# Work moved ahead of waits in a three-layer fp32 transformer kernel on one core, and decay terms on row halves

## The reference

```
# first block: eight heads of 64, T5 bias; gates; convolved feed-forward of 2816
mod = silu(c) @ ada_w + ada_b                     # 1024 x 6144, six modulation vectors
q, k, v, p, g_attn, g_pool = split((norm(x) * (1 + scale1) + shift1) @ w_in)
merged = sigmoid(g_attn) * (attn @ w_branch_attn) + sigmoid(g_pool) * (pool @ w_branch_pool)
x = x + gate1 * (merged @ w_out)
x = x + gate2 * ((silu(conv(h2 @ w_gate)) * conv(h2 @ w_value)) @ w_down)
# even layer: 8 forgetting heads and 8 sliding-window heads with sinks, then a swiglu
fq, fk, fv, fgl, sq, sk, sv = split(h @ w_in)
cum = cumsum(log_sigmoid(fgl + forget_b))         # per head, over tokens
s = fq @ fk.T / 8 + cum[query] - cum[key]         # the decay terms of a forgetting head
x = x + g_m * (concat(o_fox, o_swa) @ w_out);  x = x + g_f * swiglu(h)
# odd layer: 16 heads, each query keeps its 64 best keys by an index score, then 8 experts, top 2
q, k, v, iq, ik, iw = split(h @ w_in)             # q, k, iq, ik are rotated by position
score = sum over heads of iw * relu(iq @ ik.T);  keep top 64 keys of each query
x = x + g_m * (o @ w_out);  x = x + g_f * mixture_of_experts(h)
return rms_norm(x)
```

## Time and profile before

| | us |
|---|---|
| median of 3 runs | 1267.29 (1265.4 to 1267.48) |
| the profiled execution's own time | 1263.85 |
| span of that execution | 1262.2 |
| PE busy | 1229.3 (97%) |
| DVE busy | 671.6 (53%) |
| ACT busy | 277.8 (22%) |
| POOL busy | 88.5 (7%) |

### The profile page before, as it was taken

How to read it: one execution, slowest core, us unless ns; L and a number is a source line. 1 busy time by engine, 2 the same in 40 slices (tenths; PEclk the granted TensorE clock), 3 DMA queues, 4 the chain that set the end, 5 groups by cost and what they waited for, 6 DMA issues and landing times.

```text
span 1262.2 us, 26659 instructions
## 1 busy us (share of the span) xinstructions
PE 1229.3 (97%) x10620; PEld 936.9 (74%) x10620; DVE 671.6 (53%) x1672; ACT 277.8 (22%) x739; POOL 88.5 (7%) x157
## 2 busy tenths in 40 slices
PE   6999999999999999999999999999999999999997
PEld 4758888999999767789999997776654455455445
DVE  5455563888888735546776777883541011101104
ACT  4332203212111414540000004275300000000001
POOL 0100000000000000000000000100021100110120
PEclk9999999999999999999999999999999999999999
DMA  9999884577777583146777785795599999999993
GB/s 355 414 399 412 334 283 149 176 273 269 267 276 277 199 314 103 34 167 217 260 277 278 269 316 186 296 375 128 222 383 396 420 399 397 400 422 399 397 399 151
DMA packets 74822, 368.78 MB, mean 292 GB/s; under 512 B 8740, under 2 KB 8996, under 8 KB 49979
## 3 DMA queue, kind: packets, MB, share of 16 engines
q1 hardware_dynamic: 56594, 271.22, 57.3%
q0 software_dynamic: 18160, 96.64, 20.2%
HBM read 347.76 MB, written 20.06 MB: 291 GB/s over the span
## 4 chain that ended last, share of the span: by engine, by line
PE 92%; DVE 3%; DMA 2%; ACT 1%; SPq 1%; issue 1%; DVEq 0%
PE banks L957 21%; PE banks L697 16%; PE banks L1283 13%; PE banks L944 12%; PE banks L1332 9%; PE banks L1307 5%; PE banks L722 4%; PE banks L826 2%; PE banks L786 2%; PE banks L1024 2%; PE banks L881 1%; DMA side<-ada 1%; PE banks L865 1%; DMA ring<-stream 1%; PE banks L894 1%; DVE side L1728 1%
## 5 line engine op out<-in xcount | busy, mean ns | idle before, releaser
L1728 DVE CUSTOM_DVE_ANT_0 side<-side 128x1024 f32<-128x1024 f32 x128 | 151.1, 1220 | 32.6 <-DMA side<-ada 32.5
L1283 PE MATMUL banks<-ring,arena 128*32 128x512 f32 x1536 | 166.3, 592 | 1.6 <-DVE arena L2244 1.6
L944 PE MATMUL banks<-arena,ring 128*128 128x256 f32 x704 | 158.6, 379 | 0.0
L944 PEld LDWEIGHTS banks<-arena,ring 128*128 128x128 f32 x704 | 130.7, 190 | 16.1
L697 PE MATMUL banks<-h,ring 128*128 128x256 f32 x640 | 141.8, 380 | 0.3
L1283 PEld LDWEIGHTS banks<-ring,arena 128*32 128x32 f32 x1536 | 51.5, 110 | 111.4 <-issue 110.2
L697 PEld LDWEIGHTS banks<-h,ring 128*128 128x128 f32 x640 | 120.4, 190 | 18.4 <-issue 2.2
L2347 DVE TENSOR_TENSOR arena<-arena,banks 128x256 f32<-128x256 f32 (+1 forms) x48 | 15.2, 330 | 179.0 <-ACT arena L1665 178.9
L697 PE MATMUL banks<-arena,ring 128*128 128x256 f32 x384 | 84.3, 380 | 0.7 <-ACT arena L1464 0.5
L957 PEld LDWEIGHTS banks<-h,ring 128*128 128x128 f32 x672 | 81.4, 192 | 2.2
L614 POOL DMA_DIRECT2D side<-ada x64 | 34.0, 532 | 687.7 <-DVE msum L1728 678.2
(11 more groups left out here) (332 smaller groups left out, 1553.3 us busy)
## 6 DMA issues: line engine op xcount, KB each, us to landing
ring<-stream SPq DMA_DIRECT2D x247, 512.0 KB, 5.5
ring<-experts SPq DMA_DIRECT2D x96, 1024.0 KB, 18.9
side<-ada POOLq DMA_DIRECT2D x64, 1024.0 KB, 7.6
side<-experts SPq DMA_DIRECT2D x24, 1024.0 KB, 20.5
arena<-experts SPq DMA_DIRECT2D x8, 1024.0 KB, 21.9
yrows<-side POOLq DMA_DIRECT2D x1, 6144.0 KB, 42.7
hrows<-side POOLq DMA_DIRECT2D x1, 5632.0 KB, 23.4
arena<-lasts SPq DMA_DIRECT2D x8, 512.0 KB, 22.2
```

The lines of the kernel that those rows point to most:

```text
L944: last = pe.matmul(banks[:, 4 + c // 2, (c % 2) * T:(c % 2 + 1) * T], ring[:, s, c * P:(c + 1) * P], hid[:, j % 2, :], start=first and c % ...
L1283: ins = pe.matmul(banks[BLOCK * j:BLOCK * (j + 1), t, :], hg[:, t, k, :], ring[:, m, (j % 2) * 512:(j % 2 + 1) * 512], start=(k == 0), sto ...
L1728: dve.tensor_tensor_reduce(weights, weights, cond[:, 0 if layer0 else 1, :], 1.0, 0.0, ALU.mult, ALU.add, accum_out=msum[:, n:n + 1]).then ...
```

## The change

1. In `raw_units`, two blocks of the second raw unit stand ahead of the norm's sums. A whole normed unit (`fq` 2, `iq` 1) stands ahead of the few columns (`fgl`, `iw`), and the next one (`fq` 3, `iq` 2) ahead of their turning; ACT's takes follow in that order.
2. The wait for the two `fv` units moves from before the scores to the first product with values.
3. The decay terms contract over 40 rows: the even head of a pair on rows 0 to 39, the odd one on rows 64 to 103, with instructions of the two heads in turn. `sel` has four columns of heads in place of eight, each with the two heads of a pair; `lf72` becomes `lfs` with 104 columns, at a place of its own.
4. PE's `attend` has one order for all three attentions: the first transpose ahead of the other units of a step, except at the last steps, where they stand ahead of it. Of the last step's units, the first goes ahead of the values, the rest behind. The last early output block is split in two halves for that. In the first attention, ACT takes the second head's exponents after the transposed copy as in the others, and its other steps follow them, save at the last steps.
5. `take_query` copies the query out of PSUM first and makes the shifted copies from SBUF.
6. `rows_turned` of the first expert pass stands ahead of the copy of `pickT`.

```
--- before.py
+++ after.py
@@ -46,6 +46,7 @@
 HIDS = 2 * BLOCKS
+FORGET = 104
 EXTRA = (2 * T) // (CAP + 1)
@@ -157,10 +158,10 @@
     add(("stat", 2))
+    add(("fq", 2), 1)
     add("fgl")
-    add(("fq", 2), 1)
+    add(("fq", 3), 1)
     add("fglT")
-    add(("fq", 3), 1)
     add_all("fk", 4)
@@ -173,10 +174,10 @@
     add(("stat", 4))
+    add(("iq", 1), 1)
     add("iw")
-    add(("iq", 1), 1)
+    add(("iq", 2), 1)
     add("iwT")
-    add(("iq", 2), 1)
     add(("iq", 3), 1)
@@ -305,10 +306,10 @@
         sqT, skT, sv = region(12, [4, T]), region(16, [T]), region(17, [2, P])
-        sel = region(18, [8, T], 72)
+        sel = region(18, [4, T], FORGET)
         lf = region(26, [3, 2, 8])
-        lf72 = region(26.25, [2, 72])
-        cum = region(27, [T], 72)
+        lfs = region(22, [2, FORGET])
+        cum = region(27, [T], FORGET)
         ropet = region(29, [3, T])
@@ -797,17 +798,19 @@
                     raw_block(a.bank, a.pos, r, k)
+                for k in range(2):
+                    raw_block(b.bank, b.pos, r, k)
                 begin(U["stat", r])
...
                     raw_block(a.bank, a.pos, r, k)
-                for k in range(2):
+                for k in range(2, 4):
                     raw_block(b.bank, b.pos, r, k)
                 norm_spread(r)
-                for k in range(2, KC):
+                for k in range(4, KC):
                     raw_block(b.bank, b.pos, r, k)
 
-            def early_out(name, moving, pairs_done, k):
+            def early_out(name, moving, pairs_done, k, columns=range(4)):
 
@@ -816,7 +819,7 @@
                     pe.wait_ge(s_o, pairs_done + k + 1)
-                    for c in range(4):
+                    for c in columns:
                         out_block(name, moving, c, k)
@@ -868,9 +871,13 @@
                     for a in pair:
-                        for lo, hi, n in ((0, HALF, HALF), (HALF, TRI, T)):
-                            ins = pe.matmul(banks[:, score_bank(a.n), lo:hi], cum[:, n - HALF:n], sel[:, a.i, 0:n],
-                                            start=False, stop=bool(lo))
+                        rows = slice(64 * a.half, 64 * a.half + 40)
+                        ins = pe.matmul(banks[:, score_bank(a.n), 0:HALF], cum[rows, 0:HALF], sel[rows, a.chunk, 0:HALF],
+                                        start=False, stop=False)
+                    for a in pair:
+                        rows = slice(64 * a.half, 64 * a.half + 40)
+                        ins = pe.matmul(banks[:, score_bank(a.n), HALF:TRI], cum[rows, HALF:T], sel[rows, a.chunk, 0:T],
+                                        start=False, stop=True)
                         ins.then_inc(s_score, 1)
@@ -887,6 +894,9 @@
                     pe.wait_ge(*taken(U["sv"]))
+                if pair[0].kind == "fox" and pair[0].i == 0:
+                    pe.wait_ge(*taken(U["fv", 0]))
+                    pe.wait_ge(*taken(U["fv", 1]))
                 if done >= 1:
@@ -904,15 +914,18 @@
                         scores(pairs[m + 1])
-                    first = heads is first_heads
-                    if 1 <= m <= len(pairs) and not first:
+                    steps = between.get(2 * m, []) + between.get(2 * m + 1, [])
+                    ahead = m + 1 >= len(pairs)
+                    if 1 <= m <= len(pairs) and not ahead:
                         transposes(pairs[m - 1][0])
-                    for step in between.get(2 * m, []) + between.get(2 * m + 1, []):
+                    for step in steps[:1] if m > len(pairs) else steps:
                         step()
-                    if 1 <= m <= len(pairs) and first:
+                    if 1 <= m <= len(pairs) and ahead:
                         transposes(pairs[m - 1][0])
...
                         values(pairs[m - 2])
+                    for step in steps[1:] if m > len(pairs) else []:
+                        step()
                     if 1 <= m <= len(pairs):
@@ -1106,22 +1119,22 @@
             raw_units(2, ("fq", 0), ("fq", 1))
+            one(("fq", 2), r=2)
             few_outputs("fgl", 2)
-            one(("fq", 2))
+            one(("fq", 3))
             few_per_token("fgl")
-            one(("fq", 3))
             feature_units("fk", 4)
...
             pe.wait_ge(s_forget, 7)
-            pe.matmul(banks[0:72, u.bank, 0:T], lf72[:, 0, :], upto, start=True, stop=False)
-            pe.matmul(banks[0:72, u.bank, HALF:T], lf72[:, 1, :], upto[:, 0:HALF], start=False, stop=True).then_inc(aux_done, 1)
+            pe.matmul(banks[0:FORGET, u.bank, 0:T], lfs[:, 0, :], upto, start=True, stop=False)
+            pe.matmul(banks[0:FORGET, u.bank, HALF:T], lfs[:, 1, :], upto[:, 0:HALF], start=False, stop=True).then_inc(aux_done, 1)
             token_unit(U["fv", 0], 0, 4, 512, release=False).then_inc(aux_done, 1)
...
             pe.wait_ge(s_raw, raw_step(2, 5))
-            for name in ("fk", 3), ("fk", 2), "cum", ("fv", 0), ("fv", 1):
+            for name in ("fk", 3), ("fk", 2), "cum":
                 pe.wait_ge(*taken(U[name]))
@@ -1134,19 +1147,20 @@
                        8: [sv_unit]}
-            for k in range(7):
+            for k in range(6):
                 m = max(5, 3 + k)
                 between[2 * m] = between.get(2 * m, []) + [early_out("eo", oT2, 4, k)]
+            between[18] = [early_out("eo", oT2, 4, 6, columns) for columns in ((0, 1), (2, 3))]
             attend(even_heads, between)
...
             raw_units(4, ("ik", 0), ("iq", 0))
+            one(("iq", 1), r=4)
             few_outputs("iw", 4)
-            one(("iq", 1))
+            one(("iq", 2))
             few_per_token("iw")
-            one(("iq", 2))
             one(("iq", 3))
@@ -1192,9 +1206,10 @@
             between = {2 * (c - 4): [dq(c)] for c in range(4, 8)}
-            for k in range(7):
+            for k in range(6):
                 m = max(4, 3 + k)
                 between[2 * m] = between.get(2 * m, []) + [early_out("oo", dqT, 12, k)]
+            between[18] = [early_out("oo", dqT, 12, 6, columns) for columns in ((0, 1), (2, 3))]
             attend(odd_heads, between)
@@ -1448,15 +1463,16 @@
                         exps(pairs[m][0])
-                        if first:
-                            exps(pairs[m][1])
-                    if first:
+                    if first and m + 1 >= len(pairs):
                         for step in steps:
...
                         transposed(pairs[m - 1][0])
-                    if m < len(pairs) and not first:
+                    if m < len(pairs):
                         exps(pairs[m][1])
+                    if first and m + 1 < len(pairs):
+                        for step in steps:
+                            step()
                     if m >= 2:
@@ -1584,8 +1600,9 @@
 
+            take(U["fq", 2], fqT[:, 2, :], 0, T)
             take(U["fgl"], few, 0, T)
-            take(U["fq", 2], fqT[:, 2, :], 0, T)
+            take(U["fq", 3], fqT[:, 3, :], 0, T)
             act.wait_ge(s_forget, 1)
@@ -1594,7 +1611,6 @@
             act.activation(flat[:, 1], flat[:, 1], ACT.Ln, bias=1.0).then_inc(s_forget, 1)
-            take(U["fq", 3], fqT[:, 3, :], 0, T)
             for c in range(4):
@@ -1607,11 +1623,11 @@
 
+            take(U["iq", 1], iqT[:, 1, :], 0, T)
             take(U["iw"], few, 0, T)
-            take(U["iq", 1], iqT[:, 1, :], 0, T)
+            take(U["iq", 2], iqT[:, 2, :], 0, T)
             take(U["iwT"], iws.rearrange("p a n -> p (a n)"), 0, 16, scale=float(8 ** -0.5 * 64 ** -0.5))
-            for c in range(2, 4):
-                take(U["iq", c], iqT[:, c, :], 0, T)
+            take(U["iq", 3], iqT[:, 3, :], 0, T)
             for c in range(2):
@@ -1626,12 +1642,12 @@
                 u = U["dq", c]
-                act.wait_ge(*u.done)
+                take(u, dqT[:, c, :], 0, T)
+                act.wait_ge(*taken(u))
                 act.wait_ge(s_rope, 10 + c)
...
                     to, at = slice(BLOCK * j, BLOCK * (j + 1)), slice(BLOCK * (j ^ 1), BLOCK * (j ^ 1) + BLOCK)
-                    act.activation(ropet[to, c % 3, :], banks[at, u.bank, 0:T], ACT.Copy, scale=1.0 if j % 2 else -1.0).then_inc(s_shift, 1)
-                take(u, dqT[:, c, :], 0, T)
+                    act.activation(ropet[to, c % 3, :], dqT[at, c, :], ACT.Copy, scale=1.0 if j % 2 else -1.0).then_inc(s_shift, 1)
 
@@ -1823,7 +1839,6 @@
                 dve.tensor_tensor(part, part, sin[:, :], ALU.mult).then_inc(s_rot, 1)
-                dve.wait_ge(*taken(U["dq", c]))
                 dve.tensor_tensor(tile, tile, cos[:, :], ALU.mult).then_inc(s_rot, 1)
@@ -2057,7 +2072,7 @@
             raw_units(2, ("fq", 0), ("fq", 1), fqT[:, 0, :], fqT[:, 1, :])
-            dve.memset(lf72, 0.0).then_inc(s_cum, 1)
+            dve.memset(lfs, 0.0).then_inc(s_cum, 1)
             dve.memset(cum, 1.0).then_inc(s_cum, 1)
@@ -2070,16 +2085,22 @@
             dve.wait_ge(s_cum, 2)
```

(27 more changed lines are left out.)

## The result

The changed kernel takes 1252.16 us (median of 4 runs, 1251.21 to 1252.52) against 1266.89 of the kernel before in the same comparison: ratio 0.9884, 95% interval [0.9867, 0.9901]. The forecast was 1252.9 us, in a range of 1249 to 1259. The profiled run took 1252.16, with a span of 1250.6: 11.6 us less than the span of before.

A forecast was written before the change was run, and what follows sets the result against it. PE, busy for 97% of the span, was taken to set the time nearly everywhere. Nine terms summed to 14.4 us less: 1249.45 us in the profiled frame, 1252.9 in the median's, range 1249 to 1259.

The forecast's parts named there:

- Term 1: First attention: reordered transposes remove a 0.67 us wait, leaving 0.3 us of cover; gain 0.7, bounds 1.0 gain to 2.5 loss.
- No new wait near 119: First attention, sign in the profile after: PE would not newly wait at the later transpose, about 119.5 us.
- Terms 2 to 4 and 9: Gains: even-layer entry 2.5 us, wait for the values 0.9, decay terms 3.2, first expert pass 1.5.
- Term 9: First expert pass: turning the rows before the pick copy removes PE's 1.62 us wait; gain 1.5, bounds 1.6 and 0.
- Term 4: Decay terms: on opposite row halves a pair takes a score pair's 0.65 us, not 1.51; gain 3.2, bounds 3.7 and 0.
- Terms 5 and 6: Even and odd attention tails: fewer copy waits, one output copy still late by 0.7 and 0.35; gains 1.2 and 1.5 us.
- Rival B: ACT and DVE keep the attention tails and odd entry: tail gains 0.6 each, entry 0, total 1256.0 us; chance 0.12.
- Term 7: Odd-layer entry: PE gains 2.5 us, but DVE's chain moves only 1.5; gain 1.6, bounds 2.5 and 0.
- Term 8: First odd output block: copying query 7 first frees its bank and removes PE's 1.30 us wait; gain 1.3.
- Rival C: Expert passes: weight loading sets the pace, so the first pass's 1.5 us returns as a wait; 1254.4 us, chance 0.05.
- The clock: Granted clock is 1.00 (2.4 GHz) in both stages cited; no edit opens a longer PE gap, so nothing was charged.
- The frame: Sum made against the profiled 1263.85 us gives 1249.45; 3.44 added for the timed median 1267.29 gives 1252.9.

The follow-up runs named there:

- the repeats: The kernel before and the changed kernel, each run again without an edit: 1265.02 us and 1250.64 us, ratio 0.9880.
- the run that shifts first: Changed kernel with queries 0 to 3 shifted from PSUM first and copied out after, queries 4 to 7 still copied first: 1249.69 us.
- head by head: Changed kernel with decay terms still on opposite row halves, but both instructions of one head before both of the other: 1253.90 us.
- late rotations: Changed kernel with DVE's rotations of the first three queries two search rounds later at the odd entry: 1252.04 us.
- The run with a unit sooner: Changed kernel with one modulation unit moved on DVE ahead of the first pair's probabilities in the first attention: 1257.76 us.

## Why the prediction was right, step by step

- **The bound** held: PE's row is the time. Each term was a wait or a trickle on that row, and the nine sum to 14.0 of a forecast 14.4, and to 13.9 in the repeats.
- **Term 1** came near its 0.7 partly by luck. The first step gave 0.91, near the bound of 1.0, and the second lost 0.30, because the 0.3 us of cover there wasn't: the probabilities of the third pair came 0.27 after PE asked (0.38 in the repeat). "No new wait near 119" failed by that much.
- **Terms 2 to 4 and 9** are within 0.2 us. Term 9's wait of 1.62 is gone in every run with the change, but its 1.70 and 1.41 hold what pass 0 varies from run to run. Term 4's working by score pairs is confirmed by the run on 72 rows (3.11). Of its parts, the one on what comes next (0.15 at three places) can't be told from these rows.
- **Terms 5 and 6:** that ACT's last exponents would hold up one output copy in each tail was the step most open to doubt; the waits came at 0.62 and 0.44 where 0.7 and 0.35 were forecast, and vanish when the copy goes first. Rival B would have left terms 5 and 6 at 0.6 each.
- **Term 7** was mis-sized in the first pair of profiles: 1.29 for 1.6, and its own steps (1.9, less 0.4) give 1.5. PE did gain its 2.4; DVE's pace took 0.54 of it (0.37 in the repeat) and the wait at the first transpose 0.51. Of that wait 0.44 is ACT's new order, by the run that shifts first.
- **Term 8** was 0.17 short: it held the wait alone, and the run from the last transpose to the block shrank from 1.85 to 0.38.
- **Rival C** isn't seen: from pass 1 to the combination of rows both profiles take 300.0 us. Pass 0 is longer by 0.9 us or more in some runs, of both kernels; what it waits for there is open, so C isn't excluded for that pass.
- **The clock** is the part that failed. "No edit opens a longer gap on PE, so I charge nothing for it" overlooks that a stretch of short matmuls and waits can lose its clock in one run and keep it in the next: 1.64 us in the profiled run, nothing in the repeat.
- **The frame:** adding 3.44 for the median was sound only on average. Profiled runs of before were 1263.85 and 1265.02, medians 1265.20 to 1267.29. The changed kernel's profiled run had lost 2.4 us where the first profile of before had not, which is why the forecast of 1249.45 in the profiled frame missed by 2.7. That of the median missed by 0.7: 0.4 because the median of before was 1266.89 in the comparison and not 1267.29, the rest because the medians differ by 14.7 and not 14.4. (By the prediction's own numbers the full terms give 1251.0, not 1251.1.)

## What to carry to other kernels

Where one engine is busy for 97% of the time, list its waits with what stands ready behind each; a sum over such moves can come within half a microsecond, if for each one you name the next thing to come late and follow that engine's instructions in order. The waits that were left had each moved to the order of ACT or DVE, and three more moves of that kind gave another 2 us in the profiles. Before you believe a difference of 2 us between two profiles, compare the same stretches in a repeat of each.

## What the runs showed of the hardware

- **The granted clock in the gather.** Of 14 profiled runs three (the changed kernel's, head by head, late rotations) had the gather at a lower clock, taking 5.4 to 7.0 us for 3.78. Ahead of it PE had two waits of about 0.5 us among matmuls of 8 columns, as in the other eleven. The Trainium skill, "TensorE: Matmul & The Clock Gate", Part 1: The HAM clock gate, says that the engine's activity releases the throttle, and that the number of slow matmuls at a kernel's start varies between runs of the same kernel. The run with a unit sooner, where the clock fell behind a wait of 4.79 us, agrees with the first. The second is said of a start; here, in the gather, two runs of the changed kernel differ as well (5.41 and 3.78 us).
- **The first expert pass** took 43.9 to 44.1 us in six of the 14 (with the wait that the change removes taken off) and 0.9 to 1.5 more in the other eight, the unchanged kernel's repeat among them; some show a wait without a named releaser, such as this in the run with output copies first. The cause is open.

```profile
933.27 0.59 PE L1347 MATMUL banks<-side,arena 128*32 128x256 f32 x2 [0.69 <-issue]
```

- **Order on row halves** matters little: 0.65 us a pair when the heads alternate, 0.66 when they don't, and about 0.1 more before what follows at three places.
